# Output projection in 512 columns by halves of the inner dimension, tokens normed in order with their sums made later, and earlier operands for the down projection

## The reference

```python
mix = jnp.concatenate([o_sb, o_hg], axis=-1).astype(dt) @ w_out
h = h + mix
u2 = rmsnorm(h, norm2_g)
ffn = (jax.nn.silu(u2 @ w_gate) * (u2 @ w_up)) @ w_down
return h + ffn
```

## Time and profile before

| | us |
|---|---|
| median of 3 runs (lowest, highest) | 1410.84 (1410.66, 1414.07) |
| the profiled execution | 1416.32 |
| its span | 1414.6 |
| PE busy | 1331.5 (94% of the span) |
| DVE busy | 816.9 (58%) |
| ACT busy | 550.7 (39%) |
| POOL busy | 44.0 (3%) |

### The profile page before, as it was taken

How to read it: one execution, slowest core, us unless ns; L and a number is a source line. 1 busy time by engine, 2 the same in 40 slices (tenths; PEclk the granted TensorE clock), 3 DMA queues, 4 the chain that set the end, 5 groups by cost and what they waited for, 6 DMA issues and landing times.

```text
span 1414.6 us, 23813 instructions
## 1 busy us (share of the span) xinstructions
PE 1331.5 (94%) x9812; PEld 1116.2 (79%) x9812; DVE 816.9 (58%) x1351; ACT 550.7 (39%) x1015; POOL 44.0 (3%) x64
## 2 busy tenths in 40 slices
PE   5999999999999999689859999999999998999997
PEld 5898989897667667489858888888888876888886
DVE  5376776773787475932467655665566545435423
ACT  6323233222575555921354333333333324324411
POOL 3000000000000000010140000000000000000000
PEclk8999999999999999999989999999999999999999
DMA  6211111010010000040312222122222129615601
GB/s 196 60 31 31 31 31 32 31 53 9 2 47 16 31 2 27 6 165 31 116 64 89 87 85 82 64 86 90 89 90 90 60 82 370 213 65 201 237 23 60
DMA packets 79548, 112.24 MB, mean 79 GB/s; under 512 B 3776, under 2 KB 57024, under 8 KB 79440
## 3 DMA queue, kind: packets, MB, share of 16 engines
q1 hardware_dynamic: 77728, 104.94, 22.3%
q0 software_dynamic: 1712, 5.78, 1.1%
HBM read 90.78 MB, written 19.92 MB: 78 GB/s over the span
## 4 chain that ended last, share of the span: by engine, by line
PE 89%; ACT 5%; DVE 2%; DMA 2%; issue 2%; SPq 1%; ACTq 0%; DVEq 0%; POOLq 0%
PE ps L1912 10%; PE ps L1915 10%; PE ps L1914 10%; PE ps L313 8%; PE ps L315 8%; PE ps L314 8%; PE ps L1985 5%; PE ps L1986 5%; PE ps L1987 5%; PE ps L997 3%; PE ps L325 2%; PE ps L326 2%; PE ps L327 2%; PE ps L960 2%; PE ps L601 2%; PE ps L977 2%
## 5 line engine op out<-in xcount | busy, mean ns | idle before, releaser
L313 PE MATMUL ps<-a_hi,w_hi 128*128 128x352 f32 (+2 forms) x576 | 208.2, 362 | 7.7 <-DVE a_lo L429 3.2
L314 PE MATMUL ps<-a_lo,w_hi 128*128 128x352 f32 (+2 forms) x576 | 200.5, 348 | 0.0
L315 PE MATMUL ps<-a_hi,w_lo 128*128 128x352 f32 (+2 forms) x576 | 200.4, 348 | 0.0
L313 PEld LDWEIGHTS ps<-a_hi,w_hi 128*128 128x128 f32 x576 | 109.5, 190 | 20.5 <-DVE a_lo L429 3.6
L315 PEld LDWEIGHTS ps<-a_hi,w_lo 128*128 128x128 f32 x576 | 109.5, 190 | 8.4
L314 PEld LDWEIGHTS ps<-a_lo,w_hi 128*128 128x128 f32 x576 | 109.7, 190 | 7.3
L1912 PE MATMUL ps<-a_hi,w_hi 128*128 128x512 f32 x288 | 112.7, 391 | 2.6 <-DVE a_lo L1631 2.6
L1985 PE MATMUL ps<-a_hi,w_hi 128*128 128x512 f32 x288 | 112.1, 389 | 2.2 <-DVE a_lo L1776 2.2
L1915 PE MATMUL ps<-a_hi,w_lo 128*128 128x512 f32 x288 | 112.8, 392 | 0.0
L1914 PE MATMUL ps<-a_lo,w_hi 128*128 128x512 f32 x288 | 112.7, 391 | 0.0
L1987 PE MATMUL ps<-a_hi,w_lo 128*128 128x512 f32 x288 | 112.0, 389 | 0.0
(11 more groups left out here) (262 smaller groups left out, 2660.9 us busy)
## 6 DMA issues: line engine op xcount, KB each, us to landing
w_raw<-in_w_in_dram SPq DMA_DIRECT2D x24, 512.0 KB
w_raw<-in_w_gate_dram SPq DMA_DIRECT2D x11, 1024.0 KB, 5.6
h_res<-in_w_up_dram SPq DMA_DIRECT2D x11, 1024.0 KB, 5.4
f_spill<-h_res SPq DMA_DIRECT2D x44, 256.0 KB, 2.0
h_norm<-f_spill SPq DMA_DIRECT2D x44, 256.0 KB, 4.3
...
```

The source lines that it names most:

```text
L313: nc.tensor.matmul(psum, wh, ah, start=k == 0, stop=False)
L314: nc.tensor.matmul(psum, wh, al, start=False, stop=False)
L315: last = nc.tensor.matmul(psum, wl, ah, start=False, stop=k == KT - 1)
```

## The change

**Output projection.** A chunk of `w_out` is now 512 columns of one half of the inner dimension. O0 and O1 give the first 512 output columns, O2 and O3 the others. A group is 12 matmuls of 512 columns (`out_part`), there are again 32, and the results of eight token tiles stay in all eight banks from one chunk to the next. DVE adds 16 times 512 columns instead of 32 times 256. The transposes start after the third group of the last chunk.

**Second norm.** The tiles are finished in order 0 to 7. ACT copies each turned row out of the banks (`y_kept`) beside its high parts. T1 is made for each pair of tiles. T2, T3 and T4 are three subtractions of 128 x 2048 each on DVE (`token_sum`), after all tiles. The low parts of T2 move from POOL to DVE, those of T1 too; POOL keeps T3 and T4.

**First products.** The order of the first 13 changes, so that P6, P7 and P4, which need T2, T3 and T4, come last. PE takes the last three transposes between P1(0), P2(0) and P1(1).

**Down projection.** The first result blocks and rows of `w_down` go to other buffers, free earlier. SP issues the load for step 0 ahead of a wait, and those for steps 2 and 3 ahead of the stores of chunk 21. The eight loads of `h_back` go to POOL's queue, one for every second step. On ACT `hold_p5` stands ahead of the first operands of the down projection.

The core of the diff (indentation reduced):

```diff
-PAIRED = [0, 4, 1, 5, 2, 6, 3, 7]
-PRODUCTS = [("P1", 0), ("P2", 0), ("P1", 1), ("P2", 1), ("P5", 0), ("P6", 0), ("P5", 1), ("P7", 0), ("P6", 1),
-            ("P4", 0), ("P3", 0), ("P7", 1)]
+PRODUCTS = [("P1", 0), ("P2", 0), ("P1", 1), ("P2", 1), ("P5", 0), ("P5", 1), ("P3", 0), ("P3", 1), ("P6", 0),
+            ("P6", 1), ("P7", 0), ("P7", 1), ("P4", 0)]
 for _n in range(2, CHUNKS_GU):
-    PRODUCTS += [("P1", _n), ("P4", _n - 1), ("P3", _n - 1), ("P5", _n), ("P6", _n), ("P2", _n), ("P7", _n)]
+    PRODUCTS += [("P1", _n), ("P4", _n - 1)] + [("P3", _n - 1)] * (_n > 2) + \
+        [("P5", _n), ("P6", _n), ("P2", _n), ("P7", _n)]
 PRODUCTS += [("P4", CHUNKS_GU - 1), ("P3", CHUNKS_GU - 1)]
 NO = {key: m for m, key in enumerate(PRODUCTS)}
+LAST = {n: max(m for m, key in enumerate(PRODUCTS) if key[1] == n) for n in range(CHUNKS_GU)}
...
+Y11, Y21 = y_first[:, :, T0], y_first[:, :, T1]
+Y12, Y22 = h_res[:, UNIT:, T0], h_res[:, UNIT:, T1]
...
-down_raw = [w_raw[:, 0:D], w_raw[:, D:2 * D], h_res[:, 0], h_res[:, 1]]
-f_raw = held[0]
+held_row = h_norm[:].rearrange("p a b -> p (a b)")
+down_raw = [w_raw[:, D:2 * D], held_row[:, HALF:3 * HALF], h_res[:, 0], h_res[:, 1]]
+f_raw = [w_raw[:, 0:HALF], w_raw[:, HALF:D], held_row[:, 0:HALF]]
...
+OUT_BANKS = [0, 1, 2, 3, 4, 6, 5, 7]
...
+def out_part(slot, k0, cols, psum):
+    for k in range(UNIT):
+        c = slice(k * HALF, (k + 1) * HALF)
+        wh, wl = w_hi[:, slot, c], w_lo[:, slot, c]
+        ah, al = tok_hi[:, k0 + k, cols], tok_lo[:, k0 + k, cols]
+        opens, closes = k0 == UNIT and k == 0, k0 == 0 and k == UNIT - 1
+        nc.tensor.matmul(psum, ah, wh, start=opens, stop=False)
         nc.tensor.matmul(psum, ah, wl, start=False, stop=False)
+        last = nc.tensor.matmul(psum, al, wh, start=False, stop=closes)
...
-parts = [(dst, w_out_v[:, :, j * CW:(j + 1) * CW])]
+parts = [(w_raw[:].rearrange("p (k n) -> p k n", k=UNIT),
+          w_out_v[:, UNIT * (1 - j % 2):UNIT * (2 - j % 2), X_PARTS[j // 2]])]
...
-for i in range(5):
-    spill_h(i)
-sp.wait_ge(n2_normed.sem, n2_normed.done(3))
+for t in range(4):
+    spill_h(t)
+sp.wait_ge(n2_normed.sem, n2_normed.done(2))
...
 for n in range(2, CHUNKS_GU):
-    sp.wait_ge(block_lo.sem, block_lo.done(NO["P3", n - 2] + 1))
+    sp.wait_ge(block_lo.sem, block_lo.done(LAST[n - 2] + 1))
     load_raw(n)
     if n % 2:
         store_f(n - 2)

-sp.wait_ge(block_lo.sem, block_lo.done(NO["P3", CHUNKS_GU - 2] + 1))
+sp.wait_ge(block_lo.sem, block_lo.done(LAST[CHUNKS_GU - 2] + 1))
+load_down(0)
 for w in weighed:
     sp.wait_ge(w.sem, w.done(CHUNKS_GU - 1))
-load_down(0)
 load_down(1)
-store_f(CHUNKS_GU - 1)
 sp.wait_ge(block_lo.sem, block_lo.done(len(PRODUCTS)))
 load_down(2)
 load_down(3)
-sp.wait_ge(product_done.sem, product_done.done(len(PRODUCTS)))
-for t in range(TT):
-    sp.wait_ge(x_came[t].sem, 32)
-    sp.dma_start(h_back[t], h_spill[t * P:(t + 1) * P, :]).then_inc(x_came[t].sem, 16)
+store_f(CHUNKS_GU - 1)
...
+def low_t(src, hi_, lo_, first, done):
+    for t in range(UNIT):
+        c = slice(t * P, (t + 1) * P)
+        pool.wait_ge(t_high.sem, t_high.done(first + t + 1))
+        nc.gpsimd.tensor_tensor(lo_[:, :, c], src[:, t].rearrange("p (k n) -> p k n", k=UNIT),
+                                hi_[:, :, c].bitcast(F32), ALU.subtract).then_inc(done.sem, 1)
+low_t(Y12, t3_hi, t3_lo, UNIT, t3_done)
+low_t(Y22, t4_hi, t4_lo, 2 * UNIT, t4_done)
+pool.wait_ge(product_done.sem, product_done.done(len(PRODUCTS)))
+for t in range(TT):
+    pool.wait_ge(x_came[t].sem, 32)
+    pool.wait_ge(step_done.sem, step_done.done(2 * t + 1))
+    pool.dma_start(h_back[t], h_spill[t * P:(t + 1) * P, :]).then_inc(x_back[t].sem, 16)
...
+def high(t):
+    act.wait_ge(n2_turned.sem, n2_turned.done(t + 1))
+    if t >= UNIT:
+        act.wait_ge(x_came[t].sem, 32)
+    for b, k in enumerate((K0, K1)):
+        if b or t < UNIT:
+            nc.scalar.activation(tok_hi[:, k, t * P:(t + 1) * P],
+                                 bank(2 * (t % 2) + b).rearrange("p (k n) -> p k n", k=UNIT),
+                                 ACT.Copy).then_inc(y_high.sem, 1)
+        nc.scalar.activation(turned_rows(t)[:, X_PARTS[b]], bank(2 * (t % 2) + b), ACT.Copy)\
+            .then_inc(y_kept.sem, 1)
...
+hold_p5(n)
 if last:
     f_high(0)
     down_high(0)
...
+def low(t):
+    c = slice(t * P, (t + 1) * P)
+    if t >= UNIT:
+        dve.wait_ge(y_kept.sem, y_kept.done(2 * t + 1))
+        y11 = Y11[:, t - UNIT]
+        nc.vector.tensor_tensor(y11, Y12[:, t - UNIT], y11, ALU.subtract).then_inc(t1_ready.sem, 1)
+    for b, k in enumerate((K0, K1)):
+        if b or t < UNIT:
+            dve.wait_ge(y_high.sem, y_high.done(2 * t + b + 1 if t < UNIT else UNIT + t + 1))
+            dve.wait_ge(y_kept.sem, y_kept.done(2 * t + b + 1))
+            nc.vector.tensor_tensor(tok_lo[:, k, c],
+                                    turned_rows(t)[:, X_PARTS[b]].rearrange("p (k n) -> p k n", k=UNIT),
+                                    tok_hi[:, k, c].bitcast(F32), ALU.subtract).then_inc(y_low.sem, 1)
...
+def token_sum(n):
+    dst, a, b = ((Y11, Y22, Y11), (Y12, Y22, Y12), (Y22, Y21, Y11))[n]
+    if n == 0:
+        dve.wait_ge(y_kept.sem, y_kept.done(2 * TT))
+        dve.wait_ge(t1_done.sem, t1_done.done(UNIT))
+    else:
+        dve.wait_ge(t_ready.sem, t_ready.done(n))
+    nc.vector.tensor_tensor(dst, a, b, ALU.subtract).then_inc(t_ready.sem, 1)
...
+def out_group(c, t):
+    if c == 0 and t < 4:
+        pe.wait_ge(m_lo.sem, 2 * UNIT)
+    if c == 1 and t == 0:
+        pe.wait_ge(m_lo.sem, 4 * UNIT)
+    if t == 0:
         pe.wait_ge(w_low.sem, w_low.done(CHUNK_NO["O", c] + 1))
+    if c == 2:
+        pe.wait_ge(o_add.sem, o_add.done(t + 1))
+    out_part(c % 2, UNIT * (1 - c % 2), TOKEN_TILES[t], bank(OUT_BANKS[t])).then_inc(o_proj.sem, 1)
...
+def second_transposes(t):
+    s = t % 2
+    pe.wait_ge(n2_normed.sem, n2_normed.done(t + 1))
+    if t < 2:
+        pe.wait_ge(o_add.sem, o_add.done(TT + 2 * t + 2))
+    else:
+        pe.wait_ge(y_kept.sem, y_kept.done(2 * t - 2))
...
+if c == 3 and t == 2:
+    second_transposes(0)
+if c == 3 and t >= 4:
+    second_transposes(t - 3)
...
+second_transposes(5)
 p1(0)
+second_transposes(6)
 p2(0)
+second_transposes(7)
 p1(1)
 p2(1)
 p5(0)
+p5(1)
+p3(0)
+p3(1)
 p6(0)
-p5(1)
+p6(1)
 p7(0)
-p6(1)
+p7(1)
 p4(0)
-p3(0)
-p7(1)
 for n in range(2, CHUNKS_GU):
     p1(n)
     p4(n - 1)
-    p3(n - 1)
+    if n > 2:
+        p3(n - 1)
...```

The new order of calls on two engines, written out by hand in the change (a plain list, `bh` for `block_high`, `bl` for `block_low`):

```

More of the change, by code:

```diff
@@ L1727, in _ @@
[L1727 to L1740 removed]
+                low_chunk(dve, ("O", 1))
@@ L1741, in _ @@
+                low_chunk(dve, ("O", 2))
+                for t in range(TT):
+                    add(0, t)
+                low_chunk(dve, ("O", 3))
+                dve.wait_ge(gain2.sem, 16)
+                block_low(0)
+                block_low(1)
+                add(1, 0)
                 weight_sums(0)
                 weight_sum4(0)
+                add(1, 1)
+                scale(0)
+                add(1, 2)
+                scale(1)
+                low(0)
+                add(1, 3)
```

383 lines of the change are left out of this document (182 added, 201 removed).

## The result

The changed kernel takes 1391.73 us (median of 4 runs, 1388.97 to 1393.71) beside 1411.13 for the kernel before: a ratio of 0.9857, 95% interval 0.9835 to 0.9878. So it is 19 to 24 us faster, where 19.8 had been predicted. The profiled execution took 1388.97 us with a span of 1387.2.

What follows compares the result with a forecast made beforehand. PE, busy 94% of the span, was taken as the bound, so fewer PE cycles or holes win time. Gains of 10.5 (columns, first seam, clock) and 9.3 (second seam) make 19.8 us: 1391 for the median, range 1380 to 1401.

Steps and rivals of the forecast that it cites:

- Columns: Output projection: matmuls of 512 columns instead of 256 save 5.1 us on PE, bounds 4 to 5.5.
- Covers at nothing: Output projection: DVE's adds, the chunks' high and low parts and their loads lie beside PE's work and cost nothing.
- First seam: Output projection to gate and up projection: stalls 17.2 us against 18.5; gain 10.5 with columns and clock, bounds 4 to 24.
- P1(0) 5.1: First seam: PE waits 5.1 us before P1(0) for DVE's add 7, behind low 3 and ACT's high 3.
- P1(2) 6.8: First seam: a new 6.8 us stall before P1(2), which overwrites P4(0)'s bank, after POOL's low parts and DVE's 6.6 us.
- Clock 2.5 lost: First seam: lower clock costs PE 2.5 us, between 0 and 7, where it cost about 5.8 before.
- Second seam: Start of the down projection: earlier loads remove holes and slow matmuls, gain 9.3 us, bounds 1.7 and 9.3.
- whoever is second waits in full: Rival, 10%: in the first seam POOL's low parts wait for whole DVE instructions, 15.7 us instead of 12.6; total 1394.
- The late loads stay late: Rival, 12%: at the down projection's start only 1.7 us is gained, as loads still land late; 1398.6 for the profiled execution.
- the norm hides: Rival, 10%: first-seam hand-offs overlap better, stalls under 6 us and no low clock; total 1377.
- slower: Rival, 4%: PE's clock falls to 1.2 GHz for the whole first seam, 42 us more; total 1431.
- it does nothing: Rival, 4%: first-seam stalls reach 22 us, clock as before, down projection loads late; total about 1407.5.

Runs made afterwards that it cites:

- x_after: The changed kernel run again without any edit, in a later set: ratio 0.9833 to the kernel before.
- a_halfcols: The changed kernel with each 512-column matmul of the output projection issued as two of 256: ratio 0.9869 to the kernel before.
- d_p4_swap: The changed kernel with product P4(1) ahead of P1(2) and the weighing that frees P4(0)'s bank moved forward: ratio 0.9792 to the kernel before.

## Why the prediction was right, point by point

The time, 1391.0 for 1391.7, is right, and its two parts are right in kind. That it fits so closely is in part luck: the holes of the first seam were put 4.3 us too high, what the clock loses there 1.4 too low, and two measurements of the kernel differ by some 3 us. Summed like for like, from the first output group to the last matmul, before has 796.0 us and `x_after`, which also starts at the lower clock, 774.3: 21.8 gained, 19.8 predicted.

1. *Columns.* Predicted 5.1; 5.1 by the pace of both forms (0.240 a pair, 0.2267), while the ratios of `a_halfcols` leave 1.7 or 5.1 open. The 1.0 us that the Trainium skill's gap of a lone matmul gives (page TensorE: Matmul & The Clock Gate, Back-to-back issue gap) does not hold for this stream of matmuls, where 512 columns take 0.2267 us and 256 take 0.120.
2. *Covers at nothing.* No wait of PE in the projection other than its start: 67.88 busy of 68 us from 622 to 690. Held.
3. *First seam.* Predicted: 14th product 10.5 us nearer with the clock. Measured against `x_after` (148.9 for 163.1): 14.2, and 2.4 us of half clock follow behind P1(2), so 11.8. The terms:
   - First transposes 0.6: no wait. Seventh row 0.5: none.
   - P1(0) 5.1: this is the step that failed most. It was 2.44 + 0.89 = 3.3, and the first part was put down to the wrong thing. The sixth row wanted its bank, which ACT's kept copies of the fourth free; add 7, for which the 0.89 us wait, ended 99.5 us behind the first output group in `x_after` and not 101.2. I had priced ACT's and DVE's steps in series with 0.2 us a hand-over and ACT at 0.5 to 0.6 a copy; its copies start 0.48 us apart, and more of them overlap than I let them.
   - P5(0) 3.2: 1.4, the same over-pricing. P3(0) 1.0: 0.42. P7(0), not foreseen: 0.56.
   - P1(2) 6.8: 7.15. The cause, the hand-over without cover behind DVE's 6.6 us, was right, and `d_p4_swap` shows it. The step in front of it was wrong: I had ACT wait for GpSimd's eight pieces until 751.4, 140.6 us behind the first output group. They ended at 744.6 (136.7 behind it; 138.7 in `x_after`), and the wait that ended last was the raw weights' load at 745.1, released by P4(0)'s low part at 739.7. My sum had left this load out.
   - Clock 2.5 lost: 12 matmuls of P1(2) and about 7 of P1(0) at 0.43 instead of 0.227, 3.9. Sum 12.9 of holes for 17.2. My two ways to the gain, 10.5 and 9.7, were never made to agree; the measured 11.8 is nearer the first.
4. *Second seam.* Predicted 9.3. All holes gone, clock 1.00; undoing the part costs 8.5. The load for step 2 goes out at 1128.3, where before, shifted by the first seam's 19.1 us, it would have been 1145.1. I had added the three holes as if each had a cause of its own; the halves undone singly bring back 5.2 of the 8.5, and the clock falls only when both are undone.

Of the rivals, *whoever is second waits in full* had the mechanism right. The durations fit a GpSimd piece that waits for the DVE instruction under way and then takes its own 1.3 us (GpSimd's timeline in the changed kernel):

```profile
732.43 3.33 POOL L1320 TENSOR_TENSOR t_lo<-h_res,t_hi 128x512 fp32r<-128x512 f32 x1
...
735.73 1.74 POOL L1320 TENSOR_TENSOR t_lo<-h_res,t_hi 128x512 fp32r<-128x512 f32 x1
...
742.07 1.30 POOL L1320 TENSOR_TENSOR t_lo<-h_res,t_hi 128x512 fp32r<-128x512 f32 x1
```

beside a sum of 2.3 us, between low parts of 0.6, and beside two of DVE's additions that read one operand from a bank. The trace agrees with the rule of the Trainium skill's page SBUF — State Buffer (Who interferes with whom), that the second is blocked for the whole instruction, to within 0.3 us: 1.27 and 2.3 make 3.6, and 1.27 and 0.6 make 1.9, where 3.33 and 1.74 are measured. The eight took 13.75 us, between the 12.6 that I used (my order had them end 13.4 behind their start) and the rival's 15.7. But T4 was not what P1(2) waited for last, so its step to 1394 fails; and the larger effect was on the other side, three low parts of DVE that take 1.78 us where they take 0.69 alone, which puts off the raw weights by an estimated 3.3 us. *The late loads stay late*, *the norm hides*, *slower* and *it does nothing* are out: no hole is left in the second seam, and 12.9 us of holes are neither under 6 nor over 22. The clock fell for short stretches only. (*Slower* had its sum too high: the 59 us at 0.43 for 0.2267 make 112 and not 118.)
